# Places of matmul operands in on-chip memory: the second low weight buffer and the activations of the first block

## What is computed

```python
# first block
mod = silu(c) @ w_ada + b_ada                       # 2048 x 12288, for one row
h = rms_norm(x, g_attn_pre) * (1 + scale_a) + shift_a
proj = h @ w_in                                     # 2048 x 5456
mixed = concat(differential_attention, indexed_sparse_attention) @ w_o   # 2048 x 2048
x = x + gate_a * rms_norm(mixed, g_attn_post)
h = rms_norm(x, g_ffn_pre) * (1 + scale_f) + shift_f
x = x + gate_f * rms_norm((silu(h @ w_gate) * (h @ w_up)) @ w_down, g_ffn_post)   # width 5632
# second block, on 16 meta tokens and the 256 tokens
h = concat(meta_tokens, x)
proj = rmsnorm(h) @ w_in_2                          # 2048 x 3904
h = h + concat(neighbourhood_attention, latent_attention) @ w_out_2
h = h + (silu(conv3(rmsnorm(h) @ w_gate_2)) * (rmsnorm(h) @ w_up_2)) @ w_down_2
return h[:, 16:]
```

## Time and profile before

| | us |
|---|---|
| median of 3 runs (lowest, highest) | 2583.48 (2576.24, 2583.70) |
| the profiled execution's own time | 2583.03 |
| its span, first to last instruction | 2581.2 |
| TensorE matmul busy | 2475.4 |
| VectorE busy | 1439.2 |
| ScalarE busy | 1032.2 |
| GpSimd busy | 292.0 |

### The profile page before, as it was taken

How to read it: one execution, slowest core, us unless ns; L and a number is a source line. 1 busy time by engine, 2 the same in 40 slices (tenths; PEclk the granted TensorE clock), 3 DMA queues, 4 the chain that set the end, 5 groups by cost and what they waited for, 6 DMA issues and landing times.

```text
span 2581.2 us, 45664 instructions
## 1 busy us (share of the span) xinstructions
PE 2475.4 (96%) x18966; PEld 2296.1 (89%) x18966; DVE 1439.2 (56%) x1918; ACT 1032.2 (40%) x1332; POOL 292.0 (11%) x372
## 2 busy tenths in 40 slices
PE   6999988989999999999989998999999999999999
PEld 4999847979999999999979997778899999998877
DVE  3687657966674444444455555655655555554443
ACT  3533244344434343333334335443444444443332
POOL 5000122410100000011113002103000000000000
PEclk8999989989999999999989999999999999999999
DMA  9887864977786555555554451324455555554553
GB/s 353 290 288 268 286 211 168 337 271 237 249 294 200 184 185 189 178 185 186 179 146 149 139 160 54 126 71 131 132 188 185 179 179 179 180 185 169 193 202 131
DMA packets 263858, 504.18 MB, mean 195 GB/s; under 512 B 17152, under 2 KB 26283, under 8 KB 263467
## 3 DMA queue, kind: packets, MB, share of 16 engines
q1 hardware_dynamic: 257899, 494.97, 57.3%
q10 hardware_dynamic: 5840, 7.52, 0.9%
HBM read 498.04 MB, written 2.10 MB: 194 GB/s over the span
## 4 chain that ended last, share of the span: by engine, by line
PE 78%; DVE 8%; ACT 4%; issue 4%; DMA 3%; SPq 1%; ACTq 1%; POOL 1%; DVEq 0%; POOLq 0%
PE bank L2115 21%; PE bank L2117 20%; PE bank L2116 20%; ACT w_hi L932 3%; DVE w_lo L1462 3%; PE bank L2798 3%; PE bank L2796 3%; PE bank L2797 3%; PE bank L2150 1%; DMA raw<-in_w_in 1%; DVE ada_acc L1490 1%; DVE tmp L1596 1%; SPq L643 1%; PE bank L2259 1%; DMA staged<-in_w_ada 1%
## 5 line engine op out<-in xcount | busy, mean ns | idle before, releaser
L1462 DVE TENSOR_TENSOR w_lo<-raw,w_hi 128x2048 fp32r<-128x2048 f32 (+3 forms) x386 | 862.7, 2235 | 937.6 <-ACT w_hi L932 937.3
L2115 PE MATMUL bank<-x_hi,w_hi 128*128 128x256 f32 (+2 forms) x4608 | 1316.6, 286 | 37.1 <-DVE w_lo L1462 20.3
L2117 PE MATMUL bank<-x_hi,w_lo 128*128 128x256 f32 (+2 forms) x4608 | 1306.4, 283 | 0.0
L2116 PE MATMUL bank<-x_lo,w_hi 128*128 128x256 f32 (+2 forms) x4608 | 1300.7, 282 | 0.0
L932 ACT ACTIVATE w_hi<-raw 128x2048 fp32r<-128x2048 f32 (+3 forms) x386 | 718.7, 1862 | 1027.7 <-PE bank L2117 745.3
L2115 PEld LDWEIGHTS bank<-x_hi,w_hi 128*128 128x128 f32 x4608 | 872.2, 189 | 74.7 <-issue 41.3
L2116 PEld LDWEIGHTS bank<-x_lo,w_hi 128*128 128x128 f32 x4608 | 872.0, 189 | 1.2 <-issue 1.2
L2117 PEld LDWEIGHTS bank<-x_hi,w_lo 128*128 128x128 f32 x4608 | 871.8, 189 | 0.0
L2117 PE MATMUL bank<-hid_hi,w_lo 128*128 128x256 f32 x704 | 198.5, 282 | 0.0
L2115 PE MATMUL bank<-hid_hi,w_hi 128*128 128x256 f32 x704 | 196.8, 280 | 0.9 <-DVE w_lo L1462 0.9
L2116 PE MATMUL bank<-hid_lo,w_hi 128*128 128x256 f32 x704 | 197.1, 280 | 0.0
(11 more groups left out here) (337 smaller groups left out, 1662.0 us busy)
## 6 DMA issues: line engine op xcount, KB each, us to landing
raw<-in_w_gate SPq DMA_DIRECT2D x88, 1024.0 KB, 5.2
raw<-in_w_up SPq DMA_DIRECT2D x88, 1024.0 KB, 5.2
raw<-in_w_ada SPq DMA_DIRECT2D x72, 1024.0 KB, 6.5
raw<-in_w_in SPq DMA_DIRECT2D x68, 1024.0 KB, 5.5
raw<-in_w_down SPq DMA_DIRECT2D x64, 1024.0 KB, 5.0
raw<-in_w_down SPq DMA_DIRECT2D x32, 768.0 KB, 4.3
beside<-in_w_ada SPq DMA_DIRECT2D x16, 1024.0 KB, 7.7
raw<-in_w_o SPq DMA_DIRECT2D x16, 1024.0 KB, 6.5
```

Of the source, the lines that this page charges most:

```text
L1462: dve.tensor_tensor(w_lo[ps][:, 0:width], raw[slot][:, 0:width], w_hi[ps][:, 0:width], ALU.subtract).then_inc(raw_free[slot], 1)
L2115: pe.matmul(out, wh[:, k, c], hi(k0 + k), start=a0, stop=False)
L2116: pe.matmul(out, wh[:, k, c], lo(k0 + k), start=False, stop=False)
L2117: ins = pe.matmul(out, wl_[:, k, c], hi(k0 + k), start=False, stop=z)
```

## The change

The second low weight buffer, w_lo1, begins 64 bytes later, and with it x_res and x_hi behind it. The 64 free bytes between x_hi and x_lo are taken out, so that x_lo and all behind it stay where they were. A new helper, spaced(), lays two further sets of 16 tiles of 256 columns over the room of x_hi and x_lo, with 1024 bytes a tile and a start of its own for each group of four tiles: xin_hi and xin_lo, written by the norm attn_pre and read by the first block's input projection, and xff_hi and xff_lo, written by the norm ffn_pre and read by its gate and up. The pairs in its calls are the start of the high and the low group modulo 256, counted from byte 2208. A helper tiles() hands them to dense. All other products go on with x_hi and x_lo. No instruction, wait or transfer is added or taken out.

```diff
--- before.py
+++ after.py
@@ -231,7 +231,8 @@
             return ctx.enter_context(nc.semaphore(name))
 
 
-        cursor = [2208]
+        first = 2208
+        cursor = [first]
 
         def place(name, shape, dt=F32, at=None):
             size = 4 * int(np.prod(shape[1:]))
@@ -249,13 +250,25 @@
 
         raw = [place(f"raw{i}", [P, UK * COLS]) for i in range(RAW)]
         w_hi = [place(f"w_hi{i}", [P, UK * COLS], F32R) for i in range(SPLIT)]
-        w_lo = [place(f"w_lo{i}", [P, UK * COLS], F32R) for i in range(SPLIT)]
+        w_lo = []
+        for i, gap in enumerate((0, 64)):
+            cursor[0] += gap
+            w_lo.append(place(f"w_lo{i}", [P, UK * COLS], F32R))
         x_res = place("x_res", [P, KT, N2])
         x_hi_at = cursor[0]
         x_hi = place("x_hi", [P, KT, N2], F32R)
-        cursor[0] += 64
         x_lo_at = cursor[0]
         x_lo = place("x_lo", [P, KT, N2], F32R)
+
+        def spaced(name, phases):
+
+            tiles = []
+            for part, start in enumerate((x_hi_at, x_lo_at)):
+                tiles.append([place(f"{name}{part}_{k}", [P, S], F32R, at=start + 4 * S * k + 256 * (k // 4) +
+                                    (phases[k // 4][part] - (start - first)) % 256) for k in range(KT)])
+            return tiles
+        xin_hi, xin_lo = spaced("xin", [(64, 64), (128, 128), (192, 192), (0, 128)])
+        xff_hi, xff_lo = spaced("xff", [(0, 192), (0, 0), (64, 192), (0, 64)])
         branch_f = place("branch_f", [P, KT, S], at=x_hi_at)
         xmeta = place("xmeta", [META, D], at=x_lo_at)
         arena = cursor[0]
@@ -451,7 +464,7 @@
         kpe = proj2[0:64, T2_KPE, :]
         kpg = proj2[0:64, T2_CQ, :]
         norm("attn_pre", S, D, [[x_res[:, t, 0:S] for t in range(KT)]],
-             [(0, x_res[:, t, 0:S], gain[:, 0, t:t + 1], x_hi[:, t, 0:S], x_lo[:, t, 0:S],
+             [(0, x_res[:, t, 0:S], gain[:, 0, t:t + 1], xin_hi[t][:, :], xin_lo[t][:, :],
                mod[:, SH_A + t:SH_A + t + 1]) for t in range(KT)], True, given=x_sum)
         norm("diff", S, P, [[dout[:, h, :]] for h in range(8)],
              [(h, dout[:, h, :], lamv[:, 7:8], x_hi[:, h, 0:S], x_lo[:, h, 0:S], None) for h in range(8)], True)
@@ -459,7 +472,7 @@
              [(0, branch_a[:, t, :], gain[:, 1, t:t + 1], branch_a[:, t, :]) for t in range(KT)], False,
              branch_a_ssq, direct=4)
         norm("ffn_pre", S, D, [[x_res[:, t, 0:S] for t in range(KT)]],
-             [(0, x_res[:, t, 0:S], gain[:, 0, t:t + 1], x_hi[:, t, 0:S], x_lo[:, t, 0:S],
+             [(0, x_res[:, t, 0:S], gain[:, 0, t:t + 1], xff_hi[t][:, :], xff_lo[t][:, :],
                mod[:, SH_F + t:SH_F + t + 1]) for t in range(KT)], True, column=True)
         norm("ffn_post", S, D, [[branch_f[:, t, :] for t in range(KT)]],
              [(0, branch_f[:, t, :], gain[:, 1, t:t + 1], branch_f[:, t, :]) for t in range(KT)], False,
@@ -2126,6 +2139,10 @@
                     up.at += 4
                 else:
                     t.at += 4
+
+            def tiles(hi, lo):
+
+                return (lambda k: hi[k][:, :]), (lambda k: lo[k][:, :])
 
             def xs(n):
                 return (lambda k: x_hi[:, k, 0:n]), (lambda k: x_lo[:, k, 0:n])
@@ -2336,7 +2353,7 @@
                 if n in (0, 2, 4, 6):
                     ada_quarter(ADA_IN1 + 2 * part, n // 2)
                 ur.at = in1_unit(part, n)
-                dense([K16[part]], TAIL1 if in1_width(n) < COLS else FOUR, *xs(S), S, width=in1_width(n),
+                dense([K16[part]], TAIL1 if in1_width(n) < COLS else FOUR, *tiles(xin_hi, xin_lo), S, width=in1_width(n),
                       banks=lambda m: in1_bank(u, m), lag=IN1_BANKS,
                       tile_ready=None if u else "attn_pre")
                 if n == 6:
@@ -2594,12 +2611,12 @@
             spread("ffn_pre")
 
             def mlp1(i, tile_ready=None, ada_block=None):
-                dense(K16, FOUR, *xs(S), S, tile_ready=tile_ready,
+                dense(K16, FOUR, *tiles(xff_hi, xff_lo), S, tile_ready=tile_ready,
                       step=2 if ada_block is not None else (lambda j: 9 if j == 0 else 1) if tile_ready else 1)
                 if ada_block is not None:
                     pe.wait_ge(up_freed, up.value(4))
                     ada_sum(ada_block, bank[7])
-                dense(K16, FOUR, *xs(S), S, base=4, bank7=None if ada_block is None else ada_block + 1)
+                dense(K16, FOUR, *tiles(xff_hi, xff_lo), S, base=4, bank7=None if ada_block is None else ada_block + 1)
             mlp1(0, "ffn_pre")
             loop(4, (8, 4, 12, 4), lambda i: mlp1(i + 1, ada_block=i + ADA_MLP1))
             loop(6, (8, 4, 8, 4), lambda i: mlp1(i + 5))
```

## The result

| | before | after |
|---|---|---|
| median, us | 2583.01 (2576.24 to 2584.33) | 2587.59 (2583.51 to 2591.01) |
| the profiled execution, us | 2583.03 | 2586.10 |
| its span, us | 2581.2 | 2584.3 |

The changed kernel takes 1.0021 times as long, 95% interval 1.0013 to 1.0029: a small loss, about 5 us, where 8 us less were forecast.

What follows compares the result with a forecast made beforehand. TensorE's matmul start-to-start distance was taken as the bound. From 2583.0 us, less 4.6 (gate/up), 1.1 (input projection) and 2.0 (258 columns), came 2575.3, say 2575 us; likeliest range 2569 to 2578, outer range 2560 to 2593.

Steps and rivals of the forecast that it cites:

- the sign of the step in gate/up: Block 1's gate/up: each of 4224 matmuls 1.1 ns shorter, 4.6 us gained; called the weakest step of the sum.
- The nearest row in form: Profile of block 1's down: tiles 1024 bytes apart, one place for all, high 64 and low 128, at 117.8 ns.
- The most favourable bound: Whole fixed part of each matmul goes: 3.3 ns x 4224 = 13.9 us in gate/up, 6.8 us in the projection.
- Rows 5 and 7: Profile stretches of block 1's gate/up and block 2's up: same layout, 256 columns, yet 116.7 against 117.8 ns a matmul.
- The input projection: Block 1's 2064 projection matmuls: 1.1 ns shorter each, half counted, 1.1 us gained.
- The fear itself: In the input projection, what TensorE gains may be spent waiting for w_in to land, so half was counted.
- The 258-column stages: Block 2's gate and output projection: 0.7 ns less for each of 2880 matmuls, 2.0 us gained.
- All else at zero by symmetry: Other stages with moved x_hi or w_lo1: only the order of distances shifts, zero taken, bounds 6.4 us to either side.
- B: Rival, chance 0.21: successive moving tiles at one place cost 1.1 ns a matmul, 2594 us; gate/up units above 5.63 us.
- A: Rival, chance 0.17: no effect, sequence entry and not places sets each matmul's fixed part; 2583 us.
- C: Rival, chance 0.15: gain in gate/up alone, given back in the projection and block 2; 2578.4 us.
- D: Rival, chance 0.14: larger gain, most of the grouped stages' fixed part and 1 to 2 ns at 258 columns; 2566 us.

Runs made afterwards that it cites:

- the runs at (192, 192): Against the kernel before, block 1's input-projection and gate/up tiles at (192, 192), w_lo1 unmoved: 2573.4 us; hidden tiles there too: 2565.2; output projection also: 2561.2.
- the sharing alone: Against the kernel before, x_hi and x_res 64 bytes later so x_hi and x_lo share places, no groups, w_lo1 unmoved: 2589.4 us, ratio 1.0026.
- the eight-pair run: Against the changed kernel's groups without its 64-byte shift, eight other (high, low) pairs in gate/up and input projection, both low weight buffers at 0: 2590.0 us, one run.

## Why the prediction was wrong

**What bounds the kernel** was read rightly: TensorE's distance from start to start, a stage at a time, and 99% busy in gate/up. No other engine and no transfer came in; ScalarE's waits for TensorE and for w_in are 752.3 and 58.5 us, for 745.3 and 58.8 in the earlier trace rows. Writes to the moved tiles cost nothing that shows: from the output projection's last matmul to gate/up's first, with the norm that writes xff between them, it is 27.8 us before and 27.7 after.

**The step that failed** is the sign of the step in gate/up. I put -1.1 ns a matmul, from the thought that a place kept for a whole unit could be a good one each time. Measured: 116.7 to about 117.8, +3.5 us for the stage where -4.6 stood. The nearest row in form argued against the change with exactly this number, and I overruled it with an argument that had no row. The thought itself isn't false. Constant places can be good, but among the 16 pairs only 2 have a course below 116.6, and the change uses neither in gate/up. "Can be chosen well" is no evidence that it was. The most favourable bound, the whole fixed part of 3.3 ns gone, is close to the quick course (116.7 - 113.3 = 3.4), but that is luck: its 0.443 ns a column came from two stages with the sides changed, whose paces themselves go by places (113.3 or 117.8 ns, and 228.9 to 233.3).

**Rows 5 and 7** (one layout, two paces) I took rightly as a sign that entry matters; the runs at (192, 192) show it plainly, and so do the stretches at 116.7 and 117.8 ns in gate/up of the kernel before. But I drew from it that places might matter little. The table shows 113.3 to 121.2 ns, and among its slower courses alone still 117.1 to 121.2: a larger span than the 1.1 ns that I put as a bound.

**The input projection**, -1.1 us: measured +0.4 (stage length). There was no gain that the landing of w_in could have taken: its units at 113.3 ns, most of them with (192, 192), and those with (128, 128), at 118.6 and in the second slot up to 120.0, cancel out. The fear itself wasn't idle. In the five kernels with all its groups at (192, 192) and w_lo1 at 0 the mean distance there was 114.3 to 115.2 ns in place of 117.3, worth 4.3 to 6.1 us, and the stage got 0.3 to 3.4 us shorter. Part of the gain was lost again in each; what took it isn't shown.

**The 258-column stages**, -2.0 us: measured 0.6 us more in gate of block 2 and 0.2 in its output projection. The cause is w_lo1's place more than the sharing: with the sharing alone the gate stage takes 492.0 us, against 491.9 before and 492.5 after. **All else at zero by symmetry**: wrong in principle. High and low tiles sharing their place costs up to 1.6 ns where it is alone (at 258 columns next to nothing), and the order in which distances come up counts, not only which come up. It stayed small in sum. The input projection of block 2 lost 0.5 us (2 us with the sharing alone, so that w_lo1's 64 bytes seem to give some back there), and its down 0.8, which is w_lo1's, for its hidden tiles didn't move and with the sharing alone it takes 249.2 us. No stage of this kind moved by the 1 ns a matmul that I had named as the sign of being wrong. (For the second slot of block 2's down I put 352 matmuls, where half of its 1056 would be 528; they carried no price.)

**Rivals.** B named sharing a place as the mechanism and a unit above 5.63 us as its sign; units are at 5.66, and the loss for sharing is shown by its own run. B's price was about right for gate/up (1.1 ns), partly by luck, for only one of the four pairs there shares a place, and (0, 192), which doesn't, is at 117.7 as well. It was too high in sum (11 us for about 5): the projection lost 0.4 us and not 2.3, the other stages that read x_hi and x_lo about 1.7 and not 4.0. The measured time lies inside the outer range of 2560 to 2593, but in B's part of it and on the far side of the kernel before, so the range is no support for the forecast. As a general rule B is wrong too: the two best pairs share a place. A is right that entry sets a pace, and falls as the whole cause: a 64-byte move alone makes the kernel 0.26% slower, and steady paces run from 113.3 to 121.2 ns by places. C and D would have needed a gain in gate/up.

The rule of the Trainium skill (SBUF — State Buffer, "Who interferes with whom") is that TensorE has two independent read ports, for the moving side and for weight loads, and never waits on anyone. The traces agree as far as other engines go, by the 192 distances of 112 to 115 ns beside both splitting engines. They don't agree with what I drew from it, that addresses can't matter, nor do the two sides look independent: with the moving tiles at (192, 192), low weights at 64 in place of 0 turn 113.3 or 117.8 ns into 118.2. Whether it is the two reads that meet isn't shown.

**What is open.** Which reads of TensorE meet, and at what spacing, isn't shown; the table is an observation with weights at 0. What at a pause decides the course was not tried. Most pairs and the two kinds of down were seen in one profile each.

## What to carry to other kernels

Where the matmul is the bound and matmuls follow each other without idle time, measure the start-to-start distance in a steady stretch and hold it against the shortest seen for that width; a gap of a few per cent can be a matter of addresses. Try pairs of places in one run, one pair for each unit of a loop, as the eight-pair run does, and measure each pair in the neighbourhood it will live in: effects of two shifts didn't add. And look at single units, for a mean between two courses hides that one of them is 4% better.

## What was not expected of the hardware

- Split-product matmuls of 256 columns ran steadily at 113.3 to 121.2 ns, at a granted clock of 2.4 GHz, by the places modulo 256 bytes of moving tiles and weights. 113.3 ns is 272 clocks, 16 more than there are columns; nothing steady was seen below it.
- The same addresses allowed two steady courses, 113.3 and 117.8 ns. In one profile each, 13 stretches of gate/up were quick and 5 slow at (192, 192), 3 quick and 16 slow at (64, 64).
- Moving everything by 32 bytes changed nothing (116.7 ns in both); moving w_lo1 alone by 64 brought the second slot's units from 120.0 to 117.8 at (0, 0) and (0, 64), and from 113.3 or 117.8 to 118.2 at (192, 192).
- As stationary tiles the hidden activations had a best place too: 228.9, 231.1 and 233.3 ns for 512 columns at (192, 192), (64, 128) and (64, 64).
